# Expert rows of four token tiles read while the last two expert steps run, patched by gathers, and six of eight tiles summed on TensorE

## The chip, the cores and the metric

The kernel runs on one core of one Trainium2 chip. The metric is the device time of one execution in microseconds (us), the median of several. A core has five engines: TensorE (PE in the rows; PEld is its weight load), VectorE (DVE), ScalarE (ACT), GpSimd (POOL) and SyncE (SP, which here only issues transfers). Transfers run on 16 DMA engines that all queues share.

## What is computed

One decoder layer on 1024 tokens of width 1024, in float32: an attention part, and then a mixture of 32 experts in 4 groups with two experts for each token. The part that matters here is the end of the layer:

```
    top_v, top_i = lax.top_k(e_logits, EXPERT_TOPK)
    top_w = jax.nn.softmax(top_v, axis=-1) * p_g
...
    for e in range(N_EXPERTS):
        hid = jax.nn.silu(jnp.dot(h, w_gate[e])) * jnp.dot(h, w_up[e])
        y = y + gates[:, e:e + 1] * jnp.dot(hid, w_down[e])
    return y
...
        x = x + gate_m[:, None] * y
    return rms_norm(x, g_final)
```

So each token needs two expert rows of 1024 numbers, their weighted sum with the residual row, and a norm over the row.

## The kernel before

The tokens stand as eight tiles of 128 (t = 0 to 7, `T = 8`), one token to a partition. `XT[:, t, :]` is the residual row of tile t; it lies in the buffer `X`.

**Expert steps.** The tokens are sorted by expert into 20 steps (`NSTEP = 20`, n = 0 to 19) of 128 slots each. In a step TensorE turns the gathered rows, multiplies by gate and up weights (L2006) and by down weights (L2029), and VectorE writes the result to `ysb[n % 2]` (L1519). GpSimd gathers the rows of step n+4 (`gather`, L706) and scatters the result of step n (`scatter`, L713) into the DRAM tensor `y_dram` ("expert_rows" in the trace): row S*k + token holds what the token's k-th expert gave. The weights come through a ring of six places, issued by SP in the loop over n. The place of each token (`slots`, in the diff) is worked out before the steps by `place_tokens` on VectorE, and the lists `lst` and `dst_rows` follow from it.

**The residual rows.** Six tiles of `XT` lie where weights go, so they are written out ("residual_rows") and read back by SP once the last weights of that place are used (L588; semaphore `x2_back`).

**The end.** When both scatter semaphores `y_out[0]` and `y_out[1]` say that all 20 scatters landed, GpSimd raises `rows_out`. SP waits for it, reads the two expert rows of each of the eight tiles (16 transfers of 512 KB, `yg[t][k]`, L613), and then stores each finished tile (L616). Four tiles (`mixed`, the even ones) are summed on TensorE: `add_into` (L2067) multiplies the residual tile by the identity and each expert tile by a diagonal matrix with the tokens' weights, which adds all three up in PSUM. The other four are summed on VectorE by `combine` (L1562 and L1564). Every tile is then squared on ScalarE (L1016), its factor 1/rms is made on GpSimd (`rstd`, L651 and L652), and VectorE writes the result (`finish`, L1574).

Each engine runs its own instruction list in order, and every wait stands in the code by hand; nothing is scheduled by a planner. An overflow branch for experts with more tokens than planned is skipped with this input.

## Time and profile before

| | |
|---|---|
| median of 3 runs | 1016.02 us (1015.51 to 1017.2) |
| the profiled execution's own time | 1018.29 us |
| its span in the trace | 1016.4 us |
| granted TensorE clock, mean | 0.971 of full speed |
| TensorE busy | 946.8 us, 93% of the span |
| VectorE busy | 593.9 us, 58% |
| ScalarE busy | 401.1 us, 39% |
| GpSimd busy | 117.9 us, 12% |

The span is the stretch that the trace covers; the time of the execution is 1.9 us longer, and the median of the unprofiled runs lies 2.3 us under the profiled one. Times in the rows below are counted from the start of the span. A busy share over the whole span says little about the last 60 us, which have their own limits; they are read by stretches.

### The profile page before, as it was taken

The page shows a single profiled execution, that of the slowest core. Times are in us where ns is not written, and L with a number is a line of the kernel's source. Part 1 is how long each engine was busy: PE and PEld are TensorE (multiplying, and loading weights), DVE is VectorE, ACT ScalarE, POOL GpSimd, SP SyncE. Part 2 cuts the span into 40 slices and gives each one's busy share as a digit, 9 for nine tenths or more (in the row PEclk, how much of TensorE's full clock was granted, in tenths as well). Part 3 has the DMA queues.
Part 4 walks back from the last instruction along what each step waited for, and adds up shares of the span by engine and source line. Part 5 has one row for each costly group of instructions (what it writes and reads, how often), then busy time and mean ns, then how long its engine had stood idle before and what let it go on. Part 6 is the DMA issues. An engine that isn't in the chain of part 4 may idle for free.

```text
span 1016.4 us, 14951 instructions
## 1 busy us (share of the span) xinstructions
PE 946.8 (93%) x5302; PEld 514.1 (51%) x5302; DVE 593.9 (58%) x1593; ACT 401.1 (39%) x909; POOL 117.9 (12%) x218
## 2 busy tenths in 40 slices
PE   3899999999999999999999999996699999979975
PEld 3464575444448756777766455554233433323421
DVE  2388647999999699987777234366222333212217
ACT  6131235666650488777668121212111221111113
POOL 3001000000008411110000000000111111111003
PEclk9999999999999899999999999998799999989988
DMA  9997100110111000040000421198799999999979
GB/s 325 331 358 266 42 22 23 41 42 23 41 42 27 1 1 2 1 182 9 1 2 1 186 83 63 66 368 325 278 404 421 420 420 420 419 422 420 394 291 373
DMA packets 70956, 191.96 MB, mean 189 GB/s; under 512 B 10264, under 2 KB 37200, under 8 KB 58592
## 3 DMA queue, kind: packets, MB, share of 16 engines
q1 hardware_dynamic: 62896, 173.15, 44.7%
q0 software_dynamic: 5760, 16.78, 4.2%
q10 hardware_dynamic: 2224, 1.05, 0.4%
q8 instruction: 43, 0.70, 0.3%
q14 instruction: 33, 0.27, 0.1%
HBM read 173.12 MB, written 22.04 MB: 192 GB/s over the span
## 4 chain that ended last, share of the span: by engine, by line
PE 65%; DVE 21%; DMA 6%; issue 5%; ACT 1%; POOL 1%; SPq 0%; POOLq 0%; DVEq 0%; ACTq 0%
PE PS L2006 12%; PE PS L1891 11%; DVE BIAS L1157 8%; PE PS L1784 6%; PE PS L2029 5%; PE PS L1827 5%; PE PS L1849 4%; DMA SC<-in_w_up_dram 3%; PE PS L1745 3%; PE PS L1697 3%; PE PS L1844 2%; DMA X<-residual_rows 2%; DVE X L1221 2%; PE PS L1993 2%; PE PS L1722 2%
## 5 line engine op out<-in xcount | busy, mean ns | idle before, releaser
L1697 PE MATMUL PS<-HT,X 128*128 128x512 f32 x384 | 168.8, 593 | 0.0
L2006 PE MATMUL PS<-QKV,HT 128*32 128x512 f32 (+2 forms) x640 | 131.2, 611 | 3.3 <-ACT HT L966 1.7
L870 ACT ACTIVATE X<-X,nmx 128x128 f32<-128x128 f32 (+7 forms) x128 | 98.4, 770 | 54.4 <-DVE nmx L1221 54.1
L1697 PEld LDWEIGHTS PS<-HT,X 128*128 128x128 f32 x384 | 72.5, 190 | 92.4 <-issue 92.4
L1891 PE MATMUL PS<-QKV,HT 128*128 128x512 f32 x256 | 113.7, 597 | 0.0
L1509 DVE TENSOR_TENSOR HT<-PS,HT 128x256 f32<-128x256 f32 x20 | 8.5, 424 | 153.7 <-ACT HT L974 153.7
L1157 DVE TENSOR_SCALAR_CACHE_REDUCE BIAS<-SC,tk 128x384 f32<-128x384 f32 (+3 forms) x128 | 96.4, 809 | 1.1
L853 ACT ACTIVATE X<-SC,tk 128x896 f32<-128x896 f32 x64 | 69.6, 1088 | 43.0 <-DVE tk L1145 43.0
L1784 PE MATMUL PS<-QKV 64*128 64x512 f32 (+3 forms) x384 | 81.3, 530 | 1.6 <-DVE nmx L1221 1.1
L1891 PEld LDWEIGHTS PS<-QKV,HT 128*128 128x128 f32 x256 | 47.4, 190 | 53.7 <-issue 53.6
L2029 PE MATMUL PS<-QKV,HT 128*32 128x512 f32 (+2 forms) x320 | 65.4, 595 | 1.8 <-DMA X<-in_w_down_dram 1.8
L1827 PE MATMUL PS<-ident,X 128*128 128x128 f32 x432 | 64.0, 281 | 1.9 <-DVE X L1239 1.9
L974 ACT ACTIVATE HT<-PS 128x256 f32<-128x256 f32 x20 | 7.7, 384 | 143.8 <-PE PS L2006 143.8
L2006 PE MATMUL PS<-SC,HT 128*32 128x512 f32 (+2 forms) x144 | 58.2, 607 | 6.0 <-issue 6.0
L2006 PEld LDWEIGHTS PS<-QKV,HT 128*32 128x32 f32 (+2 forms) x640 | 38.2, 121 | 49.3 <-issue 46.5
L1221 DVE CUSTOM_DVE_ANT_0 X<-PS,R 128x128 f32<-128x128 f32 (+7 forms) x80 | 50.8, 674 | 17.8 <-PE PS L1784 11.8
L2006 PE MATMUL PS<-X,HT 128*32 128x512 f32 (+2 forms) x160 | 58.8, 626 | 0.8 <-DVE HT L1528 0.8
L1827 PEld LDWEIGHTS PS<-ident,X 128*128 128x128 f32 x432 | 48.1, 142 | 10.5 <-issue 8.6
L1221 DVE CUSTOM_DVE_ANT_0 X<-PS,SC 128x1024 f32<-128x1024 f32 (+5 forms) x48 | 42.0, 887 | 17.9 <-PE PS L1784 17.8
L1784 PEld LDWEIGHTS PS<-QKV 64*128 64x128 f32 x384 | 32.4, 190 | 28.6 <-issue 20.7
L1519 DVE TENSOR_TENSOR HT<-PS,R 128x512 f32<-128x512 f32 x40 | 27.7, 692 | 30.1 <-PE PS L2029 26.9
L1844 PEld LDWEIGHTS PS<-QKV,HT 128*128 128x128 f32 x288 | 35.6, 196 | 18.1 <-ACT HT L891 9.2
(296 smaller groups left out, 1489.3 us busy)
## 6 DMA issues: line engine op xcount, KB each, us to landing
QKV<-in_w_gate_dram SPq DMA_DIRECT2D x22, 1024.0 KB
QKV<-in_w_up_dram SPq DMA_DIRECT2D x22, 1024.0 KB
QKV<-in_w_down_dram SPq DMA_DIRECT2D x22, 1024.0 KB
QKV<-in_w_ada_dram SPq DMA_DIRECT2D x8, 2048.0 KB, 13.5
QKV<-in_w_ada_dram SPq DMA_DIRECT2D x8, 1024.0 KB, 12.5
X<-in_w_in_dram SPq DMA_DIRECT2D x16, 512.0 KB, 3.8
QKV<-expert_rows SPq DMA_DIRECT2D x16, 512.0 KB, 10.7
X<-in_w_gate_dram SPq DMA_DIRECT2D x5, 1024.0 KB
```

Of the source, the lines that this page charges most:

```text
L853: act.activation(RL[:, n % 2, 0:w], SC[:, sc_off[t]:sc_off[t] + w], ACT.Sign, bias=tk[:, 4, i:i + 1].bitcast(F32), scale=-1.0, accum_out=c ...
L870: act.activation(sc, sc, ACT.Exp, bias=nmx[:, i % 4, m:m + 1], scale=-1.0, accum_out=rs[:, i, m:m + 1]).then_inc(exp_done, 1)
L1157: dve.tensor_scalar(BIAS[:, i % 3, 0:w], SC[:, sc_off[t]:sc_off[t] + w], thr.bitcast(F32)[:, i:i + 1], 0.0, ALU.is_lt, ALU.add, accum_out= ...
L1221: dve.tensor_tensor_reduce(sc_buf[i % 4][:, m, 0:w], PS[:, 2 * m:2 * m + 2, :].rearrange("p a n -> p (a n)")[:, BANK * n:BANK * n + w], aw ...
L1697: end = pe.matmul(PS[:, 2 * b + half, :], WS[:, b, j, :], HT[:, j, BANK * half:BANK * (half + 1)], start=(j == 0), stop=(j == KC - 1))
L1784: end = pe.matmul(PS[:, 2 * m + n + c0 // BANK, 0:c1 - c0], QKV[rows_m, q0:q0 + P], QKV[rows_m, k0 + c0:k0 + c1], start=True, stop=True)
L1827: end = pe.transpose(PS[:, 4 + g % 2, c0:c0 + P], sc_buf[i % 4][:, m, P * b:P * (b + 1)], ident[:, :])
L1844: end = pe.matmul(PS[:, 6 + h % 2, slot], turned_at(i)[:, g % 4, P * (b - b0):P * (b - b0 + 1)], vf[:, u * S + P * b:u * S + P * (b + 1)], ...
L1849: end = pe.matmul(PS[DH * m:DH * (m + 1), 6 + h % 2, slot], vd[:, b, v0:v0 + DH], turned_at(i)[:, g % 4, c0:c0 + P], start=(b == 0), stop= ...
L1891: end = pe.matmul(PS[:, n % 4, :], HT[:, k, P * (n // 2):P * (n // 2 + 1)], wo[:, k, BANK * (n % 2):BANK * (n % 2 + 1)], start=(k == 0), s ...
L2006: end = pe.matmul(PS[at, 2 + b, :], hgT[b][:, P * c_ + at.start:P * c_ + at.stop], WGU[w][:, c_, :, :], start=(c_ == 0), stop=(c_ == KC - 1))
L2029: end = pe.matmul(PS[at, 5 + h, :], hidT[b][:, P * c_ + at.start:P * c_ + at.stop], WDN[w][:, c_, BANK * h:BANK * (h + 1)], start=(c_ == 0 ...
```

## The change

What it does, part by part:

- **Reading ahead.** After the residual rows SP waits until scatters 0 to 17 have landed (nine on each of `y_out[0]` and `y_out[1]`; `LATE = 18`), and reads the expert rows of tiles 0 to 3 (`AHEAD = 4`, eight transfers of 512 KB, `expert_rows`). They raise `yg_ahead`. After `rows_out` only tiles 4 to 7 are read.
- **The wait of the scatters.** Scatters 18 and 19 overwrite rows that these transfers read, so GpSimd waits for `yg_ahead` ahead of scatter 18.
- **The patch.** After the last scatter has landed GpSimd issues eight gathers, two for each of tiles 0 to 3, by the index lists `late_row`: an index is the row's own one if its slot belongs to step 18 or 19, and -1, which is out of bounds and fetches nothing, if not. VectorE makes `late_row` with one more copy in `place_tokens` (three calls) and three more operations ahead of the second `route_done`.
- **Filling `y_dram` first.** Rows not yet written would be read, so SP copies `x` twice into `y_dram` (2 x 4 MB, DRAM to DRAM) while it waits for attention; GpSimd waits for these copies ahead of its first scatter.
- **Six tiles on TensorE.** `mixed` grows from (0, 2, 4, 6) to (0, 1, 6, 2, 7, 3); only tiles 4 and 5 are summed on VectorE. There are eight PSUM banks, two to a tile, so the fifth and sixth tile reuse those of the first two, and TensorE waits for their `finish`. The tiles end in the order (4, 0, 5, 1, 6, 2, 7, 3).
- Buffers, names of semaphores and the place of the scratch for the squares move too. SP's load of `out_row` waits for the second `route_done`.

The diff, without the renaming of semaphores:

```diff
@@ -359,7 +359,8 @@
                              "ht_sb", "dn_ps", "y_sb", "rows_out"))
-        yg_in = [sem(f"yg_in{i}") for i in range(T)]
+        yg_in = [sem(f"yg_in{i}") for i in range(T // 2)]
+        yg_ahead, yg_late = sem("yg_ahead"), [sem(f"yg_late{i}") for i in range(T // 2)]
         cb_done, fin_sq, fin_done, fin_out, diag_done, mix_ps = (
@@ -378,9 +379,22 @@
         gfin = BIAS[:, 2, :]
-        mixed = (0, 2, 4, 6)
-        diag = QKV[:, 17408:18432].rearrange("p (i k n) -> p i k n", i=4, k=2)
-        yg = [[QKV[:, D * (2 * i + k):D * (2 * i + k + 1)] for k in range(2)] for i in range(T)]
+        LATE = NSTEP - 2
+        AHEAD = 4
+        last = (4, 0, 5, 1, 6, 2, 7, 3)
+        mixed = (0, 1, 6, 2, 7, 3)
+        diag = HF[:, 0:12 * P].rearrange("p (i k n) -> p i k n", i=6, k=2)
+        squared = HF[:, 2048:2048 + D]
+        yg_home = [12288, 14336, 16384, 20480, 0, 2048, 4096, 6144]
+        yg = [[QKV[:, a + D * k:a + D * (k + 1)] for k in range(2)] for a in yg_home]
+        row_col = tk[:, :, :].rearrange("p a n -> p (a n)")
+        slots = row_col[:, 0:2 * T].bitcast(F32).rearrange("p (k t) -> p k t", k=2)
+        own_row = row_col[:, 2 * T:4 * T].bitcast(F32)
+        late_row = row_col[:, 0:2 * T]
+
+        def mix_bank(i):
+
+            return 2 * (i % 4)
 
@@ -512,8 +526,10 @@
             sp.dma_start(wgr[:, :, NG:NR], w_router[0].rearrange("(j p) n -> p j n", p=P)).then_inc(wgr_in, 16)
+            for k in range(2):
+                sp.dma_start(y_dram[S * k:S * (k + 1), :], x[0]).then_inc(x_in[2 + k], 16)
             sp.wait_ge(qk_done, NA)
-            sp.dma_start(wo, w_out[0].rearrange("(k p) n -> p k n", p=P)).then_inc(wo_in, 16)
+            sp.dma_start(wo, w_out[0].rearrange("(k p) n -> p k n", p=P)).then_inc(w_in_out, 16)
             for i in range(4):
@@ -570,10 +586,18 @@
                 sp.wait_ge(xg_in[i], 16)
+            sp.wait_ge(route_done, 2)
             sp.dma_start(out_row, mod_dram[:, 3 * D:4 * D].partition_broadcast(P).rearrange("p o n -> p (o n)")
...
                 down_load(sp, expert_of(w), w)
+            def expert_rows(t):
+
+                for k in range(2):
+                    row = S * k + P * t
+                    sp.dma_start(yg[t][k], y_dram[row:row + P, :]
+                                 ).then_inc(yg_in[t - AHEAD] if t >= AHEAD else yg_ahead, 16)
+
             for n in range(NSTEP + 1):
@@ -586,6 +610,12 @@
                             sp.dma_start(XT[:, t, :], x2_dram[P * t:P * (t + 1), :]).then_inc(x2_back, 16)
+                        for b in range(2):
+                            sp.wait_ge(y_out[b], 16 * (LATE // 2))
+                        for t in range(AHEAD):
+                            if t == 3:
+                                sp.wait_ge(gu_ps, LATE + 1)
+                            expert_rows(t)
             sp.wait_ge(route_done, 2)
@@ -607,12 +637,10 @@
             sp.wait_ge(rows_out, 1)
-            for t in range(T):
-                for k in range(2):
-                    row = S * k + P * t
-                    sp.dma_start(yg[t][k], y_dram[row:row + P, :]).then_inc(yg_in[t], 16)
-            for t in range(T):
-                sp.wait_ge(fin_done, t + 1)
+            for t in range(AHEAD, T):
+                expert_rows(t)
+            for i, t in enumerate(last):
+                sp.wait_ge(fin_done, i + 1)
                 sp.dma_start(out[0, P * t:P * (t + 1), :], XT[:, t, :]).then_inc(fin_out, 16)
@@ -740,9 +768,13 @@
             pool.wait_ge(route_done, 2)
+            for k in range(2):
+                pool.wait_ge(x_in[2 + k], 32)
             for n in range(NSTEP):
...
                     gather(n + 4)
+                if n == LATE:
+                    pool.wait_ge(yg_ahead, 32 * AHEAD)
                 scatter(n)
@@ -756,8 +788,14 @@
             pool.sem_inc(rows_out, 1)
-            for t in range(T):
-                pool.wait_ge(fin_sq, t + 1)
+            for i, t in enumerate(last):
+                for a in ((0, 1, 2) if i == 0 else (3,) if i == 1 else ()):
+                    for k in range(2):
+                        pool.indirect_dma_start(out=yg[a][k], out_offset=None, in_=y_dram,
+                                                in_offset=bass.IndirectOffsetOnAxis(
+                                                    ap=late_row[:, T * k + a:T * k + a + 1], axis=0),
+                                                bounds_check=2 * S - 1, oob_is_err=False).then_inc(yg_late[a], 16)
+                pool.wait_ge(fin_sq, i + 1)
                 rstd(3 * T + t, 1, D).then_inc(rstd_done, 1)
@@ -1003,17 +1041,17 @@
                                    ).then_inc(diag_done, 1)
-            for t in range(T):
+            for n, t in enumerate(last):
                 if t in mixed:
...
                     act.wait_ge(mix_ps, i + 1)
-                    whole = PS[:, 2 * i:2 * i + 2, :].rearrange("p a n -> p (a n)")
+                    whole = PS[:, mix_bank(i):mix_bank(i) + 2, :].rearrange("p a n -> p (a n)")
                 else:
-                    act.wait_ge(cb_done, t // 2 + 1)
+                    act.wait_ge(cb_done, t - AHEAD + 1)
                     whole = XT[:, t, :]
-                if t:
-                    act.wait_ge(fin_sq, t)
-                act.activation(HF[:, 0:D], whole, ACT.Square, accum_out=ss[:, 3 * T + t:3 * T + t + 1]).then_inc(fin_sq, 1)
+                if n:
+                    act.wait_ge(fin_sq, n)
+                act.activation(squared, whole, ACT.Square, accum_out=ss[:, 3 * T + t:3 * T + t + 1]).then_inc(fin_sq, 1)
 
@@ -1387,6 +1425,7 @@
                          (tile_is[:, 0:2 * n * NSTEP], low_tok, high_tok), row_is, oh_done)
+                link(dve.tensor_copy(slots[:, :, now], slot_col[:, both].rearrange("p (k t) -> p k t", k=2)))
 
@@ -1462,6 +1501,11 @@
             link(dve.tensor_copy(ovi[:, NOV:NOV + 1], ov_end[:, NE - 1:NE]))
+            link(dve.tensor_scalar(own_row, first_tok[:, :], tok1[:, 0:1], None, ALU.add))
+            flat = row_col[:, 0:2 * T].bitcast(F32)
+            link(dve.scalar_tensor_tensor(out=flat, in0=flat, scalar=float(P * LATE), in1=own_row, op0=ALU.is_ge,
+                                          op1=ALU.mult))
+            link(dve.tensor_scalar(late_row.bitcast(I32), flat, -1.0, None, ALU.add))
             dve.sem_inc(route_done, 1)
@@ -1569,23 +1613,15 @@
                     i = mixed.index(t)
-                    whole = PS[:, 2 * i:2 * i + 2, :].rearrange("p a n -> p (a n)")
-                dve.wait_ge(rstd_done, rstd_out + t + 1)
+                    whole = PS[:, mix_bank(i):mix_bank(i) + 2, :].rearrange("p a n -> p (a n)")
+                dve.wait_ge(rstd_done, rstd_out + last.index(t) + 1)
                 dve.scalar_tensor_tensor(out=XT[:, t, :], in0=whole, scalar=ss[:, 3 * T + t:3 * T + t + 1], in1=gfin,
...
 
-            combine(1)
-            finish(0)
-            combine(3)
-            finish(1)
-            finish(2)
-            combine(5)
-            finish(3)
-            finish(4)
-            finish(5)
-            combine(7)
-            finish(6)
-            finish(7)
+            for t in range(AHEAD, AHEAD + 2):
+                combine(t)
+            for t in last:
+                finish(t)
 
@@ -2064,18 +2100,21 @@
                 for h in range(2):
-                    end = pe.matmul(PS[:, 2 * i + h, :], stationary, rows[:, BANK * h:BANK * (h + 1)], start=start,
+                    end = pe.matmul(PS[:, mix_bank(i) + h, :], stationary, rows[:, BANK * h:BANK * (h + 1)], start=start,
                                      stop=stop)
...
             pe.wait_ge(x2_back, 16 * SPILLED)
-            for i, t in enumerate(mixed):
+            for i, t in enumerate(mixed[:4]):
                 if i == 2:
...
                 add_into(i, ident[:, :], XT[:, t, :], True, False)
-            pe.wait_ge(diag_done, 8)
+            pe.wait_ge(diag_done, 2 * len(mixed))
             for i, t in enumerate(mixed):
-                pe.wait_ge(yg_in[t], 32)
+                if i >= 4:
+                    pe.wait_ge(fin_done, last.index(mixed[i - 4]) + 1)
+                    add_into(i, ident[:, :], XT[:, t, :], True, False)
+                pe.wait_ge(yg_late[t] if t < AHEAD else yg_in[t - AHEAD], 32)
                 add_into(i, diag[:, i, 0, :], yg[t][0], False, False)
...
 

```

GpSimd's list from the last gather of step rows to the second `rstd`. Before (L706 gathers, L713 scatters, L651 and L652 are `rstd`; the skipped overflow branch is left out):

```order
L706 DMA HT<-h_rows,lst 128x1024 [waits t_ps]
L713 DMA expert_rows<-HT,dst_rows 2048x1024 [waits y_sb] x5
...
L651 TENSOR_SCALAR ss<-ss 128x1 [waits y_out0,y_out1,fin_sq]
L652 TENSOR_TENSOR ss<-ss,neghalf 128x1 [waits pchain]
L651 TENSOR_SCALAR ss<-ss 128x1 [waits fin_sq]
L652 TENSOR_TENSOR ss<-ss,neghalf 128x1 [waits pchain]
```

After (L734 gather, L741 scatter, L794 the patches):

```order
L734 DMA HT<-h_rows,lst 128x1024 [waits t_ps]
L741 DMA expert_rows<-HT,dst_rows 2048x1024 [waits y_sb] x3
L741 DMA expert_rows<-HT,dst_rows 2048x1024 [waits y_sb,yg_ahead]
L741 DMA expert_rows<-HT,dst_rows 2048x1024 [waits y_sb]
...
L794 DMA QKV<-expert_rows,tk 128x1024 [waits y_out0,y_out1]
L794 DMA QKV<-expert_rows,tk 128x1024 x5
L679 TENSOR_SCALAR ss<-ss 128x1 [waits fin_sq]
L680 TENSOR_TENSOR ss<-ss,neghalf 128x1 [waits pchain]
L794 DMA QKV<-expert_rows,tk 128x1024 x2
L679 TENSOR_SCALAR ss<-ss 128x1 [waits fin_sq]
L680 TENSOR_TENSOR ss<-ss,neghalf 128x1 [waits pchain]
```

The last two scatters stand behind a new wait, and eight gathers stand behind both scatters' landing.

TensorE's list at the end, after the last expert step. Before (a row is one matmul of the program, which the trace shows as two records):

```order
L2067 MATMUL PS<-X,ident 128x512 [waits x2_back]
L2067 MATMUL PS<-X,ident 128x512 x3
L2067 MATMUL PS<-X,ident 128x512 [waits rows_out]
L2067 MATMUL PS<-X,ident 128x512 x3
L2067 MATMUL PS<-QKV 128x512 [waits yg_in0,diag_done]
L2067 MATMUL PS<-QKV 128x512 x3
L2067 MATMUL PS<-QKV 128x512 [waits yg_in2]
...
L2067 MATMUL PS<-QKV 128x512 [waits yg_in6]
L2067 MATMUL PS<-QKV 128x512 x3
```

After, from the first sum on (the eight rows with the identity ahead of it are as before):

```order
L2103 MATMUL PS<-QKV,HT 128x512 [waits yg_late0,diag_done]
L2103 MATMUL PS<-QKV,HT 128x512 x3
L2103 MATMUL PS<-QKV,HT 128x512 [waits yg_late1]
...
L2103 MATMUL PS<-QKV,HT 128x512 [waits yg_late2]
L2103 MATMUL PS<-QKV,HT 128x512 x3
L2103 MATMUL PS<-X,ident 128x512 [waits fin_done]
L2103 MATMUL PS<-X,ident 128x512
L2103 MATMUL PS<-QKV,HT 128x512 [waits yg_in3]
L2103 MATMUL PS<-QKV,HT 128x512 x3
L2103 MATMUL PS<-X,ident 128x512 [waits fin_done]
L2103 MATMUL PS<-X,ident 128x512
L2103 MATMUL PS<-QKV,HT 128x512 [waits yg_late3]
```

The first two sums now wait for patches (`yg_late`), and two more tiles, each with its identity part, follow the four.

## Rows read from the trace of the kernel before

**Rows 1.** Windows: us; busy us (instructions) of PE, PEld, DVE, ACT, POOL; clock; DMA share, GB/s

```profile
958.60:968.70 10.10, 9.79 (x72) 3.72 (x72) 1.86 (x4) 0.77 (x2) 0.97 (x1) 1.00 0.98 384
968.70:974.60 5.90, 5.06 (x37) 1.52 (x35) 1.96 (x4) 2.83 (x9) 0.97 (x1) 1.00 0.82 312
974.60:981.40 6.80, 1.27 (x2) 0.76 (x3) 0.39 (x1) 0.00 (x0) 0.97 (x1) 0.76 0.42 168
981.40:989.50 8.10, 8.10 (x16) 3.35 (x16) 0.00 (x0) 0.00 (x0) 0.00 (x0) 0.78 0.85 306
989.50:1007.40 17.90, 14.39 (x33) 5.68 (x31) 14.73 (x13) 7.67 (x13) 6.14 (x12) 1.00 1.03 415
```

**Rows 2.** Timeline of SP: start, us, queue, line, transfer, count

```profile
958.58 2.96 SPq L588 DMA_DIRECT2D X<-residual_rows  x6
981.39 9.94 SPq L613 DMA_DIRECT2D QKV<-expert_rows  x16
```

**Rows 3.** Timeline of GpSimd: scatters 17, 18 and 19, [idle before, releaser]

```profile
959.98 0.97 POOL L713 DMA_INDIRECT expert_rows<-HT,dst_rows  x1 [10.56 <-DVE HT L1519]
971.40 0.97 POOL L713 DMA_INDIRECT expert_rows<-HT,dst_rows  x1 [10.44 <-DVE HT L1519]
975.77 0.97 POOL L713 DMA_INDIRECT expert_rows<-HT,dst_rows  x1 [3.40 <-DVE HT L1519]
```

**Rows 4.** The chain that ended last, three of its pieces: start, us, what

```profile
711.20 5.68 DMA HT<-h_rows,lst
...
961.07 19.01 DMA X<-residual_rows
980.13 12.94 PE PS L2067 x24
```

**Rows 5.** Timeline of TensorE, the sums at the end

```profile
980.13 9.49 PE L2067 MATMUL PS<-X,ident 128*128 128x512 f32 x16 [5.89 <-DMA X<-residual_rows]
989.46 7.03 PE L2067 MATMUL PS<-QKV 128*128 128x512 f32 x16
997.67 3.70 PE L2067 MATMUL PS<-QKV 128*128 128x512 f32 x8 [1.18 <-DMA QKV<-expert_rows]
```

**Rows 6.** Timeline: the last tile on ScalarE, GpSimd and VectorE

```profile
1010.02 1.06 ACT L1016 ACTIVATE HT<-X 128x1024 f32<-128x1024 f32 x1 [2.39 <-DVE X L1564]
...
1011.26 0.19 POOL L651 TENSOR_SCALAR ss<-ss 128x1 f32<-128x1 f32 x1 [0.87 <-ACT HT L1016]
...
1012.11 1.28 DVE L1574 SCALAR_TENSOR_TENSOR X<-X,ss,BIAS 128x1024 f32<-128x1024 f32 x1 [0.41 <-POOL ss L652]
```

**Rows 7.** Windows of 1 us, columns as in rows 1

```profile
978.00:979.00 1.00, 0.00 (x0) 0.00 (x0) 0.00 (x0) 0.00 (x0) 0.00 (x0) 0.54 0.60 242
979.00:980.00 1.00, 0.00 (x0) 0.00 (x0) 0.00 (x0) 0.00 (x0) 0.00 (x0) 0.50 0.12 49
985.00:986.00 1.00, 1.00 (x3) 0.38 (x2) 0.00 (x0) 0.00 (x0) 0.00 (x0) 1.00 1.03 344
```

**Rows 8.** Time from issue to landing: first of expert_rows, then of h_rows

```profile
DMA to landing us min/median/max: 3.7/10.7/15.0
DMA to landing us min/median/max: 2.6/8.7/13.9
```

**Rows 9.** All matmuls of the sums with diagonals: ns min/median/max, first and last start

```profile
L2067 PE MATMUL PS<-QKV x32: 592/592/697, 989.5 to 1005.9; 128*128 128x512 f32 x32
```

**Rows 10.** SP's longest wait for attention, and a window inside it (columns as in rows 1)

```profile
SPq L516 <- PE PS L1784: 118.3, 1, 118.3
340.00:370.00 30.00, 28.32 (x152) 17.61 (x151) 23.30 (x103) 22.20 (x86) 6.09 (x11) 0.83 0.00 1
```

**Rows 11.** Timelines: VectorE behind two place_tokens and the list, ScalarE at the diagonals

```profile
677.95 0.69 DVE L1432 TENSOR_TENSOR BIAS<-PS,HT 128x512 f32<-128x512 f32 x1 [1.38 <-PE PS L1891]
710.11 0.18 DVE L1448 TENSOR_SCALAR lst<-PS 128x20 int32<-128x20 f32 x1 [0.54 <-PE PS L1915]
719.08 1.37 DVE L1528 TENSOR_SCALAR HT<-PS,gm,modc 128x128 f32<-128x128 f32 x4 [6.85 <-PE PS L1993]
971.48 2.45 ACT L1004 ACTIVATE QKV<-ident,rt 128x128 f32<-128x128 f32 x8 [0.94 <-issue]
```

14 lines of the change are left out of this document (7 added, 7 removed).

## The prediction, on record before the changed kernel ran

> **What bounds the kernel now.** The change touches the last 60 us, so I looked for what is waited for there, stretch by stretch.
>
> I began with the windows [rows 1]. Until 968.7 the DMA engines are full (share 0.98). Between 974.6 and 981.4 their share is 0.42, and TensorE, VectorE and ScalarE do nothing much. From 989.5 on the DMA engines are full again at 415 GB/s. So the tail has two parts: a hole in which everybody waits for the last expert rows to be written, and a stretch in which the 16 reads and the 8 stores pass through.
>
> The timelines of SP and GpSimd give the hole its dates. The last scatter (19) is issued at 975.77 [rows 3], and SP's first read of expert rows starts at 981.39 [rows 2], which is the moment of `rows_out`. I call this moment r. Before the change r = 981.4, and from r to the end of the span it is 1016.4 - 981.4 = 35.0 us. The landing of a scatter issued into emptying queues thus took 981.4 - 975.8 = 5.6 us.
>
> The chain has a second late piece: the six residual transfers, issued from 958.58 on [rows 2], keep TensorE waiting until 980.13 [rows 4, 5]. Their landing took 19 us although they are 3 MB. The windows of 1 us show why: at 979 the share of the DMA engines is 0.12 [rows 7], so one or two of the sixteen still work while the rest are idle. The engines do not finish together; the slowest is behind, and a wait lasts until the slowest is done.
>
> Last I read TensorE's own cost. Sixteen records of the sum with diagonals take 7.03 us [rows 5]; with 0.59 us for one record [rows 9], their starts are (7.03 - 0.59) / 15 = 0.43 us apart. A tile has 8 such records (two expert rows, two banks, two records to a matmul) and 4 with the identity. Before, TensorE sums four tiles and waits for transfers between them, with 1.18 us of idle time ahead of the third [rows 5]. It is close behind the transfers, but they bound it.
>
> **The change, part by part.**
>
> *When the early reads start.* SP waits for scatter 17, issued at 959.98 [rows 3]. No row gives its landing; the gathers, which share its queue and mostly run beside weights, took 8.7 us in the median [rows 8]. So the eight reads (8 x 0.524 = 4.19 MB) are issued from about 968.7 on.
>
> *When they have landed.* Between 968.7 and 981.4 the DMA engines still moved 312 x 5.9 + 168 x 6.8 = 2983 KB, so 2.98 MB [rows 1]. In that are scatters 18 and 19 (1.05 MB), which will now come later; 1.93 MB remain and go ahead of the reads. If all engines shared the work evenly, 1.93 + 4.19 = 6.12 MB at 415 GB/s take 14.8 us, and the reads land at 983.5. That is the lower bound. By the slowest engine it is later: it finished the residual rows at 980.1; without its share of the two scatters (1.05 / 0.415 = 2.5 us) at 977.6; its share of the reads takes 4.19 / 0.415 = 10.1 us more: 987.7. Without the deduction it is 990.2, the upper bound. I take 987.7, because the idle share of rows 7 shows that here the slowest engine sets the landing.
>
> The Trainium skill, "DMA: Bandwidth & Descriptors", section "Latency and other measured facts", says that two of the sixteen engines are usually slower than the others when GpSimd's transfers are about. By that rule the sum is 987.7 and not 983.5. The trace agrees as far as one or two engines were last at 979; it does not say which.
>
> *When the last scatters have landed: the new r.* Scatter 18 had been issued at 971.40. Now it waits for `yg_ahead`, hence until 987.7, and scatter 19 stands behind it. An issue takes 0.97 us [rows 3], so scatter 19 is issued at 988.7. Its landing takes between 3.7 us (the shortest for expert rows, rows 8) and 5.6 us (above); the queues are empty this time, but two scatters are in them, so I take the middle, 4.7. The new r is 987.7 + 1.0 + 4.7 = 993.4, with bounds 983.5 + 1.0 + 3.7 = 988.2 and 990.2 + 1.0 + 5.6 = 996.8. That is **12.0 us later** than before. Behind the waiting scatter nothing but the end stands in GpSimd's queue, and no expert step needs `ysb` again, so the price is paid once.
>
> *What happens behind r.* TensorE first has the identity part of tiles 6 and 2: 8 records. It has been idle for some 8 us by then. Before, its granted clock fell to half (1.2 of 2.4 GHz) at 978, after it had been idle from 974 on, and was full again at 985, after it had worked from 980.13 on [rows 5, 7]. So the 8 records take at most 8 x 0.86 = 6.9 us. Meanwhile GpSimd issues the two gathers of tile 0 (the second starts 1.0 us after r), and they must land: 5.7 us in nearly idle queues [rows 4], 8.7 us in the median under load [rows 8]. They carry few rows, but SP fills the queues with 4 MB at the same moment; I take 7.0. The first sum starts at r + 1.0 + 7.0 = r + 8.0, with bounds r + 6.9 (the identities) and r + 1.0 + 8.7 = r + 9.7.
>
> From there TensorE has six tiles of 8 records and two identity parts of 4, 56 records in one row: 55 x 0.43 + 0.59 = **24.2 us**. Nothing need interrupt it: the patches of tiles 1 and 2 are issued 2 us apart, the reads of tiles 6 and 7 are through after 4.19 / 0.415 = 10.1 us, and tiles 0 and 1, whose banks are used again, are finished in time, since VectorE has 12 operations of 1.28 us [rows 6], 15.4 us in all, and two eight-row sums of slack. So TensorE, and no longer the transfers, sets the pace.
>
> The last tile then passes ScalarE, GpSimd, VectorE and its store. Before, this was from 1010.02 [rows 6] to 1016.4: 6.4 us.
>
> *The sum.* 993.4 + 8.0 + 24.2 + 6.4 = 1032.0 as the end of the span, against 1016.4: **+15.6 us**. With all low bounds it is 988.2 + 6.9 + 24.2 + 6.4 = 1025.7 (+9.3), with all high ones 996.8 + 9.7 + 24.2 + 6.4 = 1037.1 (+20.7). The profiled execution took 1018.29 us, 1.9 us more than its span; it would come out at 1033.9. The median of the runs is 1016.02, so I forecast 1016.0 + 15.6 = 1031.6 for the median.
>
> *Edits that I cost at nothing.* The two fills move 8.4 MB from DRAM to DRAM. SP issues them ahead of a wait of 118.3 us, in which the DMA engines are idle [rows 10]; they need 8.4 / 118 = 71 GB/s, a sixth of what rows 1 show. No row shows a transfer inside DRAM; were it four times slower than a read (104 GB/s), it would still be covered, and if the cover failed, the weights of the output projection would come later, which have another wait's time to spare. The extra copies in `place_tokens` are some 0.2 us each and lie where VectorE then waits 1.38 and 0.54 us for TensorE [rows 11]; without this cover they would cost 0.2 us each. The three operations ahead of the second `route_done` (0.6 us) lie in an idle stretch of 6.85 us [rows 11]. The four more diagonals cost ScalarE 4 x 0.31 = 1.2 us from 974 on [rows 11], where it has nothing else to do for 19 us.
>
> **The rivals.**
>
> *The tail stays bound by transfers, and the change is a gain.* 4.19 MB of reads leave the stretch behind r. The patches add at most 256 rows of 4 KB, half of which belong to tiles 0 to 3, about 0.5 MB. So 3.7 MB less at 415 GB/s: 8.9 us less, and the end is r + 35.0 - 8.9 = r + 26.1. With the lowest r, 988.2, that is 1014.3, 2.1 us **faster** than before, a median of 1013.9. It decides at r = 988.3: the early reads must be down by 983.6. For it speaks that the engines idle from 974.6 on [rows 1]. Against it: even shared evenly the reads land at 983.5, and TensorE would have to be through 19.7 us after r (r + 26.1 less the 6.4 of the last tile), whereas its records alone need 6.9 + 24.2 = 31.1 us. With the r of my sum this rival gives 1019.5, a median of 1019.1 (+3.1). Both together: 0.13, of which 0.07 for faster; 0.04 more for values between, within 0.2%.
>
> The same page of the Trainium skill, section "Rules for kernel authors", says that to overlap a transfer with compute one issues it early and waits for it late. By that rule the early reads are hidden and this rival's time, 1014 to 1019, is what comes out. Against it stands that here the wait for the early reads is not late: scatter 18 waits for them at once.
>
> *Something that I cost at nothing costs.* If the fills were not covered or disturbed the instruction streams, or if the gathers took 13.9 us to land (their maximum, rows 8) instead of 7.0, the median would be over 1037. Chance 0.05.
>
> **How the numbers follow.** What a measurement of this kernel can tell from no change is about 0.2%, 2 us. Forecast (TensorE's sums behind a late r): 0.78, its own range 1025.3 to 1036.7. Transfers bound, late r, 1019: 0.06. No change: 0.04. Faster: 0.07. Worse than 1037: 0.05. The range 1020 to 1037 leaves out about 0.17 and takes in both bounds of the sum. Slower is 0.78 + 0.06 + 0.05 = 0.89.
>
> **What would show it.** In the new trace: SP's early reads start near 968.7. Scatter 18 is issued at 984 to 990 and not at 971, scatter 19 a microsecond later, and SP's second group of reads at 988 to 997. TensorE's L2103 starts its diagonals 7 to 10 us after that and then runs 56 records with less than 2 us of gaps; the DMA share in the last 15 us is well under 1. I am wrong if scatter 18 is issued before 983, if TensorE waits for transfers or patches more than 3 us between its sums, or if anything before 958 moves by over a microsecond.

## The result, and the profile after

The changed kernel takes **1038.94 us** in the median of 4 runs (1034.61 to 1040.13), against 1015.76 us (1015.4 to 1017.2, 4 runs) for the kernel before: a ratio of 1.0217, 95% interval 1.0198 to 1.0236. The forecast was 1031.6 us with a range up to 1037. The direction was right, the slowdown was forecast 7.3 us too small, and the time lies 1.9 us above the range. The profiled execution took 1034.61 us, with a span of 1032.7 us; it was the fastest of the four.

The reading goes in the order of the prediction. First the timelines of SP and GpSimd; they answer to [rows 2] and [rows 3].

```profile
954.45 2.81 SPq L612 DMA_DIRECT2D X<-residual_rows  x6
964.41 30.32 SPq L598 DMA_DIRECT2D QKV<-expert_rows  x16
```

```profile
955.86 0.98 POOL L741 DMA_INDIRECT expert_rows<-HT,dst_rows  x1 [10.56 <-DVE HT L1563]
985.86 0.98 POOL L741 DMA_INDIRECT expert_rows<-HT,dst_rows  x1 [29.02 <-DMA QKV<-expert_rows]
987.15 0.98 POOL L741 DMA_INDIRECT expert_rows<-HT,dst_rows  x1 [0.30 <-issue]
991.44 1.04 POOL L794 DMA_INDIRECT QKV<-expert_rows,tk  x1 [3.32 <-DMA expert_rows<-HT,dst_rows]
992.79 1.02 POOL L794 DMA_INDIRECT QKV<-expert_rows,tk  x1 [0.30 <-issue]
```

Scatter 18 now stands 29.02 us in GpSimd's queue, and what releases it is the landing of the early reads. In [rows 3] it followed scatter 17 by 11.4 us and waited for VectorE. That bracket holds the larger part of the loss. The next rows show its consequences: scatter 19, then the first two patch gathers.

The end of the chain, which answers to [rows 4], links them: scatter 17 lands, the early reads land, a gather lands, and then TensorE works without a gap.

```profile
955.86 8.49 DMA expert_rows<-HT,dst_rows
968.98 16.12 DMA QKV<-expert_rows
992.79 7.43 DMA QKV<-expert_rows,tk
1000.36 25.98 PE PS L2103 x56
```

TensorE's timeline (answers to [rows 5]): identities, a wait for GpSimd, identities again, a wait for a patch, then 56 records of one row.

```profile
975.10 6.45 PE L2103 MATMUL PS<-X,ident 128*128 128x512 f32 x8 [4.87 <-DMA X<-residual_rows]
990.65 5.50 PE L2103 MATMUL PS<-X,ident 128*128 128x512 f32 x8 [9.10 <-POOLq L790]
1000.36 15.67 PE L2103 MATMUL PS<-QKV,HT 128*128 128x512 f32 x32 [4.20 <-DMA QKV<-expert_rows,tk]
1015.86 1.88 PE L2103 MATMUL PS<-X,ident 128*128 128x512 f32 x4
1017.58 3.60 PE L2103 MATMUL PS<-QKV,HT 128*128 128x512 f32 x8
...
1022.73 3.60 PE L2103 MATMUL PS<-QKV,HT 128*128 128x512 f32 x8
```

The windows (columns as in rows 1), cut at the same events:

```profile
975.10:985.90 10.80, 6.45 (x8) 2.52 (x8) 0.00 (x0) 0.00 (x0) 0.04 (x1) 0.66 0.50 201
985.90:990.70 4.80, 0.05 (x1) 0.05 (x1) 0.00 (x0) 0.00 (x0) 1.92 (x2) 0.50 0.50 201
990.70:1000.40 9.70, 5.50 (x9) 2.14 (x9) 4.28 (x4) 1.15 (x2) 6.93 (x8) 0.81 0.91 344
1000.40:1005.00 4.60, 4.60 (x7) 1.93 (x8) 2.14 (x2) 0.00 (x0) 4.11 (x3) 0.63 0.96 361
1005.00:1032.70 27.70, 21.32 (x50) 9.12 (x48) 8.91 (x7) 7.84 (x14) 5.44 (x15) 0.92 0.36 139
```

Before, the stretch from 989.50 on was full of transfers (share 1.03) [rows 1]. Now the DMA engines are at half share for 15 us ahead of the new `rows_out`, and at 0.36 in the last 27.7 us. The transfers are no longer the bound, and nothing was gained by it.

**One date that makes all traces comparable.** Traces of the same kernel differ by some microseconds long before the tail, in step with where TensorE's clock is granted at half (shown further down). So I count from the issue of scatter 17. From there to the end of the span it was 1016.4 - 959.98 = 56.4 us before [rows 3], and is 1032.7 - 955.86 = 76.8 us now: **+20.4 us**. I call this the tail. In it r is the moment of `rows_out`, read as the start of SP's plain reads or of TensorE's second identities. All entries below are differences of two starts in the traces, in us; those for the experiments belong to the next section.

| kernel | 17 to 18 | 17 to r | r to end | tail |
|---|---|---|---|---|
| before | 11.4 | 21.4 | 35.0 | 56.4 |
| after | 30.0 | 34.8 | 42.0 | 76.8 |
| e3, six tiles on TensorE, no early reads | 11.6 | 21.6 | 40.0 | 61.6 |
| e4, early reads from another tensor | 11.4 | 23.7 | 50.2 | 74.0 |
| e5, after with four tiles on TensorE | 30.0 | 34.8 | 35.5 | 70.2 |
| e6, after without patches | 29.6 | 34.4 | 36.3 | 70.7 |
| e8, two tiles ahead, four on TensorE | 25.0 | 29.8 | 36.6 | 66.4 |
| e12, before with the wait alone | 20.1 | 24.9 | 34.5 | 59.3 |

### The profile page after: what moved, and what is told of

Its sections match the earlier page's. It is cut to its first block, busy times and chain, and to the rows that moved or that the text cites. A ratio compares the mean times of both kernels' runs of the same rounds, so it can differ in the third digit from the quotient of the medians.

```text
span 1032.7 us, 15030 instructions
## 1 busy us (share of the span) xinstructions
PE 956.7 (93%) x5326; PEld 517.8 (50%) x5326; DVE 590.2 (57%) x1595; ACT 401.9 (39%) x913; POOL 125.2 (12%) x226
## 4 chain that ended last, share of the span: by engine, by line
PE 64%; DVE 20%; DMA 8%; issue 5%; ACT 1%; POOL 1%; SPq 1%; POOLq 0%; DVEq 0%; ACTq 0%
PE PS L2042 12%; PE PS L1927 10%; DVE BIAS L1195 7%; PE PS L1820 6%; PE PS L2065 5%; PE PS L1863 4%; PE PS L1885 4%; DMA SC<-in_w_up_dram 3%; PE PS L1781 3%; PE PS L1733 3%; PE PS L2103 3%; PE PS L1880 2%; DVE X L1259 2%; PE PS L2029 2%; PE PS L1758 2%
## 5 line engine op out<-in xcount | busy, mean ns | idle before, releaser
L1820 PE MATMUL PS<-QKV 64*128 64x512 f32 (+3 forms) x384 | 79.0, 517 | 1.6 <-DVE nmx L1259 1.1
L1927 PEld LDWEIGHTS PS<-QKV,HT 128*128 128x128 f32 x256 | 47.4, 190 | 53.7 <-issue 53.6
L1820 PEld LDWEIGHTS PS<-QKV 64*128 64x128 f32 x384 | 31.6, 185 | 27.8 <-issue 20.4
L1563 DVE TENSOR_TENSOR HT<-PS,R 128x512 f32<-128x512 f32 x40 | 27.7, 691 | 30.1 <-PE PS L2065 30.0
L1087 DVE SCALAR_TENSOR_TENSOR QKV<-QKV,cact 128x512 f32<-128x512 f32 x56 | 42.1, 752 | 2.0
```

The costliest lines, as they stand in the source:

```text
L1087: link(dve.scalar_tensor_tensor(out=w[:, 0, :], in0=w[:, j, :], scalar=cact[:, j:j + 1], in1=w[:, 0, :], op0=ALU.mult, op1=ALU.add))
L1820: end = pe.matmul(PS[:, 2 * m + n + c0 // BANK, 0:c1 - c0], QKV[rows_m, q0:q0 + P], QKV[rows_m, k0 + c0:k0 + c1], start=True, stop=True)
L1927: end = pe.matmul(PS[:, n % 4, :], HT[:, k, P * (n // 2):P * (n // 2 + 1)], wo[:, k, BANK * (n % 2):BANK * (n % 2 + 1)], start=(k == 0), s ...
```

## The experiments

Theory A, after the result: the early reads delay r by 13.4 us, because scatter 18 waits for them, and behind r patches and six tiles in a row on TensorE cost 7 us more than the saved transfers give back. The rivals: the fills disturb earlier stages; the wait is not what costs, since without it the reads and patches cost as much; the traces miss something that moved ahead of the tail.

**e1_again** is the changed kernel once more, with no edit, on one chip with e2, e3 and e4.

> The changed kernel itself, nothing edited, for a second trace and more times. In its first trace the stretch from the issue of scatter 17 to the end takes 76.8 us against 56.4 before (+20.4), while everything ahead of scatter 17 came 4.1 us earlier than in the trace of before. Theory A (the tail is the whole loss; what lies ahead differs only by when TensorE's clock happens to be granted at half): the new trace shows 75 to 79 us from scatter 17 to the end, and scatter 17 itself at 956 to 961; the median is 1016 + 20 to 23. Theory B (the change also delays work ahead of scatter 17, and the first trace was a lucky one): scatter 17 at 962 or later.

Measured: 1036.51 us (1033.77 to 1038.29, 6 runs), ratio 1.0212 (1.0187 to 1.0237), before at 1014.21 us there. Scatter 17 is issued at 957.77 and the tail is 77.0 us.

**e2_fills_only** is the kernel before with the two fills and GpSimd's wait for them.

```
+            for k in range(2):
+                sp.dma_start(y_dram[S * k:S * (k + 1), :], x[0]).then_inc(x_in[2 + k], 16)
...
+            for k in range(2):
+                pool.wait_ge(x_in[2 + k], 32)
```

> The kernel before, plus only the two copies of x into the expert rows (8.4 MB from DRAM to DRAM) and GpSimd's wait for them. Theory A: no change, within 1.5 us of 1016, the copies are through by 345 us. Theory B (the copies delay instruction fetches or attention and are the 2 to 3 us by which the median of the changed kernel lies above what its tail explains): 1018 to 1020.

Measured: 1016.75 us (1012.12 to 1018.68, 12 runs), before at 1014.21 us there, ratio 1.0012 (0.9995 to 1.0029); the tail is 56.5 us. So the fills cost the tail nothing, and the whole kernel nothing clear of the spread; the interval of the times alone leaves room for up to 2.9 us. What the trace of after shows fits (windows, columns as in rows 1):

```profile
314.00:342.00 28.00, 27.68 (x249) 27.13 (x247) 21.43 (x25) 2.88 (x9) 22.86 (x11) 1.00 1.01 318
342.00:430.00 88.00, 84.11 (x542) 55.98 (x543) 80.73 (x230) 74.00 (x217) 11.83 (x26) 1.00 0.00 1
```

The fills pass in 28 us, and for the 88 us that follow the queues are empty.

**e3_six_tiles_only** is the changed kernel without fills, early reads, wait, patches and their lists; the new order of tiles and the six tiles on TensorE stay. The code shows three of its edits.

```
-                        for b in range(2):
-                            sp.wait_ge(y_out[b], 16 * (LATE // 2))
...
-            for t in range(AHEAD, T):
+            for t in last:
                 expert_rows(t)
...
-                if n == LATE:
-                    pool.wait_ge(yg_ahead, 32 * AHEAD)
```

> The changed kernel without reading ahead, fills, patches or the wait of the scatters: all eight tiles are read after the last scatter landed, in the order in which they are finished, and six are summed on TensorE. Theory A (TensorE's row of sums is a bound of its own): tiles arrive every 2.6 us, but a sum takes 3.4 us and the last two another 1.7 each, so the span ends 40 to 42 us after SP's first read instead of 35.0: +5 to +7 us, 1021 to 1023. Rival (only the late last scatters cost, six tiles on TensorE are free): within 2 us of 1016.

Measured: 1022.55 us (1021.78 to 1023.76, 6 runs), ratio 1.0081 (1.0059 to 1.0103). TensorE's timeline:

```profile
988.11 3.60 PE L2079 MATMUL PS<-QKV,HT 128*128 128x512 f32 x8
992.96 10.57 PE L2079 MATMUL PS<-QKV,HT 128*128 128x512 f32 x24 [1.25 <-DMA QKV<-expert_rows]
1003.36 1.88 PE L2079 MATMUL PS<-X,ident 128*128 128x512 f32 x4
```

r stays where it was (21.6 us behind scatter 17) and r to end grows from 35.0 to 40.0 us. In the first sums TensorE still waits 1.25 us for a transfer, then never again. So two more tiles on TensorE, with the new order of tiles, cost 5 us by themselves, with as many transfers as before. The median says 8.3 us; the trace's 5.2 us lies just under its interval (6.0 to 10.4 us), and I trust the tail more, since it leaves out the spread ahead of scatter 17.

**e4_other_tensor** takes the wait away by taking away its reason: the early reads go to a tensor that no scatter writes. It leaves out the expert rows of steps 0 to 17 for tiles 0 to 3 (rows of x stand in their place).

```
-                    sp.dma_start(yg[t][k], y_dram[row:row + P, :]
+                    sp.dma_start(yg[t][k], (y_dram if t >= AHEAD else z_dram)[row:row + P, :]
...
-                if n == LATE:
-                    pool.wait_ge(yg_ahead, 32 * AHEAD)
...
             pool.sem_inc(rows_out, 1)
+            pool.wait_ge(yg_ahead, 32 * AHEAD)
```

> The changed kernel, but the early reads come from another DRAM tensor (filled with x), so that scatters 18 and 19 need not wait for them; the patches wait for the early reads instead, since they write into the same tiles. Left out: the expert rows of steps 0 to 17 for tiles 0 to 3, which are replaced by x. Theory A: scatter 18 is issued some 11 us after scatter 17 as in the kernel before, the last scatter lands and SP reads on 8 to 10 us earlier than in the changed kernel, but TensorE still starts its first sum only some 8 us after the early reads are down (29 us after scatter 17), so only 5 to 7 us of the 20.4 come back: 1031 to 1034. Rival (the wait of the scatters carries over in full to the end): 9 to 10 us come back, 1028 to 1030.

Measured: 1034.67 us (1033.4 to 1036.09, 4 runs), ratio 1.020 (1.017 to 1.023); the tail is 74.0 us. Only 2.8 of the 20.4 us come back, less than either theory said (theory A had 5 to 7 us, the rival 9 to 10). GpSimd's and TensorE's timelines show where the rest stays:

```profile
969.54 0.97 POOL L742 DMA_INDIRECT expert_rows<-HT,dst_rows  x1 [10.46 <-DVE HT L1563]
973.91 0.97 POOL L742 DMA_INDIRECT expert_rows<-HT,dst_rows  x1 [3.40 <-DVE HT L1563]
990.74 1.04 POOL L794 DMA_INDIRECT QKV<-expert_rows,tk  x1 [15.85 <-DMA QKV<-filled_rows]
```

```profile
978.56 9.35 PE L2103 MATMUL PS<-X,ident 128*128 128x512 f32 x16 [6.18 <-DMA X<-residual_rows]
999.39 16.02 PE L2103 MATMUL PS<-QKV,HT 128*128 128x512 f32 x32 [11.49 <-DMA QKV<-expert_rows,tk]
```

The scatters go out on time, but the patches overwrite rows in the same buffers, so they cannot be issued before the early reads are down, and these now land 24.3 us behind their first issue (966.48 to 990.74) instead of 21.4. The two scatters now share the engines with them, which is the likely reason and is not tested by itself. The first sum is 41.3 us behind scatter 17, against 44.5 in after. The wait in front of scatter 18 is thus not the cause by itself: **whichever instruction waits for the early reads, their landing date carries the tail.** The part of theory A that says "because scatter 18 waits" falls here.

**e5_four_on_tensor** is the changed kernel with four tiles on TensorE, as many as before.

```
-        mixed = (0, 1, 6, 2, 7, 3)
+        mixed = (0, 1, 6, 2)
+        added = (4, 5, 7, 3)
```

> The changed kernel with tiles 0, 1, 6 and 2 on TensorE and the expert rows of 4, 5, 7 and 3 added on VectorE; reads ahead, wait and patches stay. Theory A (the last stretch is TensorE's row of sums behind the patches): the row loses two tiles of 2 x 1.8 + 0.9 to 2 x 1.8 + 1.8 us, so the time is 8 to 10 us less than the changed kernel's, near 1027 to 1029, and from the issue of scatter 17 to the end it is 67 to 69 us instead of 77. Rival (VectorE, with two more tiles of adds, ends last, or the patch of tile 3 does): only 3 to 6 us less, near 1031 to 1034.

Measured: 1029.61 us (1028.0 to 1032.76, 6 runs), ratio 1.0137 (1.0112 to 1.0162), 6.9 us under e1 and e7. That is under theory A's 8 to 10 and over the rival's 3 to 6. r is as late as in after, but r to end is 35.5 us, almost before's 35.0. VectorE's timeline shows why it isn't less:

```profile
1012.40 1.28 DVE L1607 SCALAR_TENSOR_TENSOR X<-QKV,rt,X 128x1024 f32<-128x1024 f32 x1
1013.72 1.28 DVE L1609 SCALAR_TENSOR_TENSOR X<-QKV,rt,X 128x1024 f32<-128x1024 f32 x1
1015.44 1.28 DVE L1619 SCALAR_TENSOR_TENSOR X<-PS,ss,BIAS 128x1024 f32<-128x1024 f32 x1 [0.44 <-POOL ss L681]
...
1021.54 1.28 DVE L1619 SCALAR_TENSOR_TENSOR X<-X,ss,BIAS 128x1024 f32<-128x1024 f32 x1
1023.53 1.28 DVE L1619 SCALAR_TENSOR_TENSOR X<-X,ss,BIAS 128x1024 f32<-128x1024 f32 x1 [0.71 <-POOL ss L681]
```

TensorE is through at 1018.2, but from 1009.99 on VectorE has eleven operations of 1.28 us with little idle time, up to 1024.8. So VectorE, and no longer TensorE, is the engine in which work is queued up to the end.

**e6_no_patches** is the changed kernel without the eight patch gathers. The rows that the last two steps wrote for tiles 0 to 3 are left out. Shown is the wait that takes the place of the patches' own; the gathers are deleted.

```
-                pe.wait_ge(yg_late[t] if t < AHEAD else yg_in[t - AHEAD], 32)
+                pe.wait_ge(yg_ahead if t < AHEAD else yg_in[t - AHEAD], 32 * AHEAD if t < AHEAD else 32)
```

> The changed kernel without the eight patch gathers: the rows that the last two steps wrote for tiles 0 to 3 are left out of the sum, and the sums of these tiles wait for the reads ahead alone. Theory A (the first sum waits for gathers that are issued 1.3 us apart and land 7.4 us after their issue, 4.2 us past the end of the x2 sums): the first sum follows the x2 sums without a gap, and the time is 4 to 6 us less than the changed kernel's, near 1031 to 1033. Rival (the reads of tiles 4 to 7 wait in the DMA queues behind nothing and land sooner too, so that TensorE's row is no bound and the whole of the 9.7 us comes back): 8 to 10 us less. Rival (the patches are hidden behind the other reads): within 1 us.

Measured: 1029.59 us (1026.38 to 1031.78, 4 runs), ratio 1.0134 (1.0101 to 1.0168), 6.9 us under e1; the tail is 6.1 us shorter. The chain's last piece is TensorE alone, identities and sums in one row from r on:

```profile
990.97 29.91 PE PS L2097 x64
```

Even with no patch at all the kernel is 13 us slower than before. r to end is 5.7 us shorter than in after: the gap of 4.2 us is gone, and the first 32 records of the sums take 13.90 us and not 15.67, since after no gap they run at the full clock.

**e7_tensor_busy** fills TensorE's gap: the identities of tiles 6 and 2 are computed twice.

```
                     pe.wait_ge(rows_out, 1)
+                    add_into(2, ident[:, :], XT[:, t, :], True, True)
+                    add_into(3, ident[:, :], XT[:, t, :], True, True)
```

> The changed kernel with four more matrix products for TensorE in its gap ahead of the first patched sum: the x2 sums of tiles 6 and 2 are computed twice. Theory A (1.7 us of TensorE's 26.0 us were lost since its clock was granted at half from 1001.4 to 1004.8 after this gap): the clock stays whole there, and the time is 1 to 2 us less than the changed kernel's. Rival (the clock falls anyway, because of the idle time further ahead): the same time, or up to 1 us more.

Measured: 1036.54 us (1033.38 to 1038.93, 6 runs), ratio 1.0199 (1.0175 to 1.0223), the same as e1. TensorE's timeline and a window on it:

```profile
995.12 9.06 PE L2103 MATMUL PS<-X,ident 128*128 128x512 f32 x16 [9.00 <-POOLq L790]
1006.37 13.97 PE L2103 MATMUL PS<-QKV,HT 128*128 128x512 f32 x32 [2.18 <-DMA QKV<-expert_rows,tk]
```

```profile
1004.00:1008.00 4.00, 1.82 (x5) 0.87 (x5) 3.49 (x3) 0.00 (x0) 3.72 (x3) 1.00 1.04 400
```

The clock stays whole (1.00) and the first 32 records take 13.97 us instead of 15.67, so the 1.7 us are the clock's (the window covers the first 1.6 us of the sums). But in this trace the second gather landed 9.1 us behind its issue and not 7.6, so the first sum began 1.5 us later, and the tail is 76.6 us, 0.2 less than in after. Whether later gathers belong to the edit or to chance I can't tell from one trace; in the four traces with the same issues (after, e1, e5, e11) the second gather took 7.4 to 8.0 us, by the chain's rows, and here 9.0. The runs show no gain.

**e8_two_ahead** reads two tiles ahead instead of four, with four patches and four tiles on TensorE.

```
-        AHEAD = 4
+        AHEAD = 2
...
-            for t in range(AHEAD, T):
+            for t in (4, 5, 6, 2, 7, 3):
```

> Reads ahead for tiles 0 and 1 alone, four patches instead of eight, twelve plain reads at the end (4, 5, 6, 2, 7, 3 in this order), four tiles on TensorE (0, 1, 6, 2). Theory A (what the change costs is the wait of scatter 18 for its reads and the row of gathers, each in proportion to the tiles read ahead): the four reads land some 8 us sooner than eight, scatter 18 is issued about 20 us behind scatter 17 and not 29, the first sum follows some 35 us behind scatter 17, and the end some 61 to 64 us, so the time is 1019 to 1023. Rival (even four reads stand behind the weights of the last experts on the slowest DMA engine, and land when eight do): scatter 18 still 27 to 29 us behind scatter 17, and a time of 1026 to 1030. Rival on the other side (the two tiles read ahead save more at the end than the shorter wait costs): under the kernel before, below 1015.

Measured: 1026.94 us (1023.3 to 1027.78, 5 runs), ratio 1.011 (1.0085 to 1.0135). GpSimd's timeline:

```profile
980.11 0.98 POOL L740 DMA_INDIRECT expert_rows<-HT,dst_rows  x1 [24.04 <-DMA QKV<-expert_rows]
```

Scatter 18 is 25.0 us behind scatter 17: neither 20 nor 27 to 29. Four reads less (2.1 MB) bring it 5.0 us nearer, which is as much as 420 GB/s would take. Carried on to no early read at all, 20 us would remain, against 11.4 before. That gave the last experiment.

**e9_before_again, e10_before_third, e11_after_third** are further traces of both kernels, since the medians differed by 22 to 23 us and the tails by 20.4.

> The kernel before, unchanged, profiled once more. Theory A (nothing that the change does moves anything ahead of scatter 17; its issue falls anywhere between 955 and 960 us, as TensorE's clock happens to be granted at half near 30 and 346 us or not, and the first trace of before was at the late end): scatter 17 is issued at 955 to 960, and from there to the end it is 56 to 57 us. Rival (before always reaches scatter 17 at 959.5 to 960.5, and the changed kernel sooner, so that the change gains 2 us ahead of the tail): 959.5 to 960.5 here too.

> The kernel before, a third trace, with the same expectations as for the second one: by theory A at least one of the two has scatter 17 before 959; by the rival neither has.

> The changed kernel unchanged, a third trace. Theory A: scatter 17 is issued at 955 to 960, and from there to the end it is 76.5 to 77.5 us. Rival: scatter 17 always at 955.5 to 958 in the changed kernel.

Measured: 1017.29, 1016.09 and 1038.5 us. Scatter 17 in each, by GpSimd's timeline:

```profile
958.97 0.98 POOL L713 DMA_INDIRECT expert_rows<-HT,dst_rows  x1 [10.56 <-DVE HT L1519]
```

```profile
957.69 0.98 POOL L713 DMA_INDIRECT expert_rows<-HT,dst_rows  x1 [10.57 <-DVE HT L1519]
```

```profile
959.49 0.98 POOL L741 DMA_INDIRECT expert_rows<-HT,dst_rows  x1 [10.56 <-DVE HT L1563]
```

The tails are 56.4, 56.5 and 77.1 us. So before reaches scatter 17 at 957.7 to 960.0 in three traces, and after at 955.9 to 959.5 in three. The tails repeat within 0.3 us, the dates of scatter 17 do not. That the change moves them is not excluded by the ranges alone. Two pairs of traces say more, one of each kernel with the clock at the same levels in the same stretches. In e10 and e1 it is 1.00 from 0 to 60 us and 0.95 from 300 to 400, and scatter 17 comes at 957.69 and 957.77. In e9 and e11 it is 0.94 and 1.00, and scatter 17 comes at 958.97 and 959.49. So at the same clock levels no more than about 0.5 us between the kernels is left ahead of scatter 17. Windows of e1 and of e9:

```profile
300.00:400.00 100.00, 96.53 (x621) 70.23 (x622) 86.61 (x217) 51.70 (x163) 39.45 (x36) 0.95 0.29 92
```

```profile
0.00:60.00 60.00, 40.69 (x221) 23.02 (x221) 23.79 (x61) 22.05 (x35) 9.40 (x88) 0.94 1.00 328
```

**e12_wait_only** is the kernel before with one wait: scatter 18 waits for the residual rows.

```
+                if n == NSTEP - 2:
+                    pool.wait_ge(x2_back, 16 * SPILLED)
                 scatter(n)
```

> The kernel before, with one wait added and nothing moved: scatter 18 waits until the six residual transfers have landed, as it waits for the early reads in the changed kernel. It is the changed kernel's wait with no early read in it. Theory A (the floor of that wait is the slowest DMA engine's backlog of weights and residual rows; eight reads made it 30.0 us and four reads 25.0 us from scatter 17 to scatter 18, so none makes it 20): scatter 18 is issued 19 to 21 us behind scatter 17 and not 11.3, rows_out comes at 24.5 to 26.5 us and not 21.4, and the time is 2.5 to 5 us more than before's. Rival (the early reads are themselves what is slow, and the backlog is short): scatter 18 at 12 to 16 us behind scatter 17, and the time of before within 1 us.

Measured: 1018.4 us (1015.86 to 1020.17, 12 runs), before at 1016.68 (17 runs), ratio 1.0023 (1.0008 to 1.0037). GpSimd's timeline and windows ahead of the release:

```profile
957.28 0.97 POOL L713 DMA_INDIRECT expert_rows<-HT,dst_rows  x1 [10.56 <-DVE HT L1521]
977.38 0.98 POOL L713 DMA_INDIRECT expert_rows<-HT,dst_rows  x1 [19.13 <-DMA X<-residual_rows]
```

```profile
974.00:975.00 1.00, 0.00 (x0) 0.00 (x0) 0.00 (x0) 0.00 (x0) 0.00 (x0) 0.96 0.13 53
975.00:976.00 1.00, 0.00 (x0) 0.00 (x0) 0.00 (x0) 0.00 (x0) 0.00 (x0) 0.50 0.09 37
```

Scatter 18 is issued 20.1 us behind scatter 17 and r comes at 24.9 us, both as theory A says; the tail is 2.9 us longer. The median moved by 1.7 us, less than the 2.5 that I expected at least. The windows show the kind of wait: in the last microseconds ahead of the landing (976.6) the DMA engines' share is 0.13 and 0.09. Almost all of them are idle, and the wait stands for what the last one or two still have in their queues.

That is also what the Trainium skill says, "DMA: Bandwidth & Descriptors", section "Why a DMA increments its semaphore by 16 and not by 1": up to 16 engines finish independently, and only the full 16 means that all has landed. The trace agrees: share 0.13 and 0.09 in two of the last three microseconds ahead of the landing.

## Why the prediction was right in kind and too small in size

**Where the 20.4 us are.** Late r: +13.4 us. Of these, 3.5 us come from a wait for SP's queue at this point with nothing read ahead (24.9 against 21.4 us, e12), and 9.9 us the eight reads (34.8 against 24.9); e8 measured 5.0 us for four. Behind r: +7.0 us. Six tiles on TensorE alone cost 5.0 (e3), the patches 5.7 when six tiles are on TensorE (e6, r to end 42.0 against 36.3), and they overlap with each other and with what the saved transfers give back. With four tiles on TensorE, r to end is 35.5 us (e5): the late r is then all that is left of the loss.

**Step by step.** Each term of the sum, from the issue of scatter 17, as predicted and in the trace of after:

| term | predicted | measured | 
|---|---|---|
| scatter 17 lands, early reads issued | 8.7 | 8.6 |
| early reads down, scatter 18 | 19.0 | 21.4 |
| scatter 18 to r | 5.7 | 4.8 |
| r to the first sum | 8.0 | 9.7 |
| 56 records | 24.2 | 26.0 |
| last tile | 6.4 | 6.4 |

The sum is 72.0 against 76.8 (the rounded terms give 76.9), and that is 4.8 of the 7.3 us.

*The step "When they have landed"* failed in size, by 2.4 us, in two places. I had taken 2.5 us off the slowest engine for the two scatters that now come later, which puts the end of its residual rows 17.6 us behind scatter 17. Before, it was 20.1 us [rows 4]; in after TensorE, released by it, starts at 975.10, so 19.2 us, and in e12, where both scatters are held back too, 19.4. The deduction was worth 0.7 to 0.9 us and not 2.5: what left with the two scatters was far less on the slowest engine than on the average one. The reads then took what I had given them, 10.1 us: the chain has them down at 968.98 + 16.12 = 985.10, 10.0 us behind the residual rows. The second place is a term that I did not have: scatter 18 is issued 0.8 us behind that landing, at 985.86. In e12 TensorE (976.66) and scatter 18 (977.38) wait for the same semaphore, and GpSimd is 0.7 us later there too. That the total equals my value without the deduction (21.5) is a coincidence.

The slowest engine did set the date. In after the DMA engines' share is 1.03 until 978; then it falls over 7 us. The last whole microsecond ahead of the landing:

```profile
984.00:985.00 1.00, 0.00 (x0) 0.00 (x0) 0.00 (x0) 0.00 (x0) 0.00 (x0) 0.54 0.07 29
```

*The step "What happens behind r"* failed twice. I let the second gather start 1.0 us behind r; it started 2.1 us behind it (992.79 against 990.65), because the first issue comes 0.8 us behind r and issues are 1.35 us apart where I had counted their duration alone. It landed 7.6 us later where I had 7.0. And I took the records at full clock. TensorE had been idle for 4.2 us ahead of the first sum, its clock was granted at half until about 1005 (0.63 in the window), and that costs 1.7 to 1.8 us; e7, where the clock stayed whole, shows the same size. The prediction had read the fall of the clock for the identities and not applied it to the sums.

*The step from the span to the median* cost the other 2.5 us. I added the difference of the tails to the median of before. In e1's six runs that would have been right to within 2 us (1014.21 + 20.4 = 1034.6, measured 1036.51); in the first comparison the four runs of after lay higher. The tail's +20.4 us lies just inside the sum's upper bound of +20.7, so it is only by this step that the median left the range, and e1's median of the same kernel lies inside it. On which side of 1037 the result fell was chance; the 4.8 us in the sum were not. With tails that repeat to 0.3 us, spans of 1032.7 to 1038.3 us mean that scatter 17 came anywhere between 955.9 and 961.5. The part of the spread that I can name is TensorE's clock in earlier stages. Windows of after (scatter 17 at 955.86, the earliest of the six traces of the two kernels), of e11 (959.49) and of e10 (957.69), columns as in rows 1:

```profile
0.00:60.00 60.00, 40.30 (x228) 21.78 (x228) 26.62 (x65) 23.85 (x38) 9.40 (x88) 1.00 0.99 326
300.00:400.00 100.00, 95.87 (x641) 70.01 (x640) 88.84 (x220) 54.21 (x175) 39.46 (x36) 1.00 0.30 93
```

```profile
0.00:60.00 60.00, 40.45 (x221) 23.08 (x221) 23.47 (x61) 21.75 (x35) 9.41 (x88) 0.94 1.01 328
```

```profile
300.00:400.00 100.00, 96.56 (x621) 70.17 (x621) 86.64 (x217) 51.83 (x163) 39.43 (x36) 0.95 0.04 8
```

The clock (third column from the end) was whole in both stretches in after, and granted at half for a part of one of them in e11 and e10, of one kernel and of the other. That all of the spread in the unprofiled runs is of this kind is argued, not shown.

**What held.** The bound moved from the transfers to TensorE's row of sums behind a late r; the row was not interrupted; the fills were hidden (e2); the last tile took 6.4 us; the gain of early reads for the transfers was real (share 0.36 at the end) and brought no time. The rival "transfers bound, a gain" is out: even e6, with no patches, is slower by 13 us. Its condition was reads down by 983.6, that is 23.6 us behind scatter 17; e12's wait with no reads at all takes 20.1, which leaves room for about 1.4 MB. The wait of scatter 18 and the wait for the first patch both came out at my upper bounds, and the records above the one value that I had; my range took such a coincidence to be rare. It also left out more than I wrote: the chances that I gave for outcomes outside 1020 to 1037 (0.06, 0.04, 0.07 and 0.05) add up to 0.22 and not 0.17.

One of my signs of being wrong did show, and it was a bad sign to choose: scatter 17 and all ahead of it came 4.1 us earlier than in the trace of before, and I had allowed one microsecond. Traces of one kernel differ by up to 3.6 us there. Counted from scatter 17 the other signs are as forecast: scatter 18 at 30.0 us (24.0 to 30.0), the first sum 9.7 us behind r (7 to 10), and no gap in the 56 records.

No variant came out under the kernel before, and the experiments point to none: e8, the best with early reads, has a tail of 66.4 us, and e12 shows that a wait at this place costs 2.9 us before the first byte is read ahead.
